# Moving VectorE's modulation products one place up in its order, and the split of one output weight ahead of the scores of heads 4 and 5

## The reference, cut to what matters

```python
c_act = jax.nn.silu(c)
mod = jnp.matmul(c_act, w_ada[l]) + b_ada[l]                  # 1024 -> 6 * 1024
sh_m, sc_m, gt_m, sh_f, sc_f, gt_f = jnp.split(mod, N_MOD, axis=-1)
h = modulate(rmsnorm(x, norm_mix_g[l]), sh_m, sc_m)
proj = jnp.matmul(h, w_in[l])
q, k, v, f_logit, u = jnp.split(proj, split_pts, axis=-1)
log_f = jax.nn.log_sigmoid(f_logit + b_fgate[l])
attn_out = forgetting_attention(q, k, v, log_f)   # logits + cumsum(log_f)[t] - cumsum(log_f)[s]
pool_out = multiscale_pool(u, w_pool[l], pool_scale[l])
mix = jnp.matmul(jnp.concatenate([attn_out, pool_out], -1), w_out[l])
x = x + gt_m[:, None, :] * mix
```

## Time and profile before

| | before |
|---|---|
| median of 3 runs | 771.52 us (771.48 to 771.83) |
| profiled execution, its own time | 771.5 us |
| its span | 769.7 us |
| TensorE matmul busy | 689.6 us (90%) |
| VectorE busy | 357.2 us (46%) |
| ScalarE busy | 295.3 us (38%) |
| read from HBM | 208.32 MB, 272 GB/s over the span |
| mean granted clock of TensorE | 0.972 |

### The profile page before, as it was taken

One profiled execution on the slowest core, in us unless ns is written; L12 is line 12 of the kernel. 1 busy time (PEld: TensorE's weight loads), 2 busy tenths in 40 slices (PEclk: granted clock), 3 DMA queues, 4 the chain that ended last, 5 costly groups with the idle time before them and its releaser, 6 DMA issues.

```text
span 769.7 us, 13061 instructions
## 1 busy us (share of the span) xinstructions
PE 689.6 (90%) x5482; PEld 538.5 (70%) x5482; DVE 357.2 (46%) x571; ACT 295.3 (38%) x432; POOL 46.5 (6%) x84
## 2 busy tenths in 40 slices
PE   3999999899757677778999999999999999999996
PEld 3887778743323122224999989998889999999995
DVE  3568861521110110105946885535675645555443
ACT  4244430331111010005764544678255643444432
POOL 0000000000000000000073750000000000000000
PEclk9999999999999898889999999999999999999999
DMA  8999899999999999999845234314345356554001
GB/s 354 408 418 391 318 424 419 422 421 421 424 422 424 422 421 426 403 413 424 308 181 218 113 126 181 134 64 156 110 170 185 135 195 219 219 196 185 3 1 55
DMA packets 33038, 210.27 MB, mean 273 GB/s; under 512 B 4688, under 2 KB 5072, under 8 KB 8656
## 3 DMA queue, kind: packets, MB, share of 16 engines
q1 hardware_dynamic: 32976, 209.38, 68.3%
HBM read 208.32 MB, written 1.05 MB: 272 GB/s over the span
## 4 chain that ended last, share of the span: by engine, by line
PE 70%; DMA 16%; DVE 5%; SPq 3%; ACT 3%; issue 1%; DVEq 0%; ACTq 0%
PE psum L419 69%; DMA raw<-in_w_exp 12%; DMA raw<-in_w_in_t 3%; SPq L459 2%; SPq L474 1%; PE psum L427 1%; DVE wlo L512 1%; ACT whi L495 1%; DMA raw<-in_w_ada_q 1%; DVE XL L1962 0%; DVE X L2398 0%; DVE acc L534 0%; ACT G L1283 0%; DVE XT L1310 0%; ACT XT L2342 0%
## 5 line engine op out<-in xcount | busy, mean ns | idle before, releaser
L419 PE MATMUL psum<-XH,whi 128*128 128x256 f32 x736 | 210.2, 286 | 4.3 <-DVE XL L665 2.8
L419 PE MATMUL psum<-XH,wlo 128*128 128x256 f32 x736 | 208.3, 283 | 0.0
L419 PE MATMUL psum<-XL,whi 128*128 128x256 f32 x736 | 208.0, 283 | 0.0
L512 DVE TENSOR_TENSOR wlo<-raw,whi 128x2048 fp32r<-128x2048 f32 (+1 forms) x88 | 168.9, 1957 | 48.6 <-ACT whi L495 48.6
L495 ACT ACTIVATE whi<-raw 128x2048 fp32r<-128x2048 f32 (+1 forms) x79 | 139.4, 1802 | 38.9 <-PE psum L419 22.4
L419 PEld LDWEIGHTS psum<-XH,whi 128*128 128x128 f32 x736 | 139.2, 189 | 8.0 <-issue 3.5
L419 PEld LDWEIGHTS psum<-XH,wlo 128*128 128x128 f32 x736 | 138.8, 189 | 0.0
L419 PEld LDWEIGHTS psum<-XL,whi 128*128 128x128 f32 x736 | 138.6, 188 | 0.3
L419 PE MATMUL psum<-raw,G 128*32 128x512 f32 x456 | 67.7, 682 | 20.3 <-DMA raw<-in_w_exp 20.2
L419 PEld LDWEIGHTS psum<-raw,G 128*32 128x32 f32 x456 | 17.7, 123 | 57.5 <-issue 56.6
L1267 ACT ACTIVATE WT<-psum 128x256 f32<-128x256 f32 x8 | 3.1, 383 | 134.4 <-PE psum L419 98.6
(11 more groups left out here) (350 smaller groups left out, 947.1 us busy)
## 6 DMA issues: line engine op xcount, KB each, us to landing
raw<-in_w_exp SPq DMA_DIRECT2D x85, 1024.0 KB, 23.1
raw<-in_w_ff SPq DMA_DIRECT2D x32, 1024.0 KB, 5.3
raw<-in_w_in SPq DMA_DIRECT2D x22, 1024.0 KB, 6.5
raw<-in_w_ada SPq DMA_DIRECT2D x16, 1024.0 KB, 11.7
raw<-in_w_in_t SPq DMA_DIRECT2D x8, 1024.0 KB, 18.4
X<-in_w_exp SPq DMA_DIRECT2D x5, 1024.0 KB, 24.9
raw<-in_w_ada_q SPq DMA_DIRECT2D x4, 1024.0 KB, 17.3
raw<-in_w_out_t SPq DMA_DIRECT2D x4, 1024.0 KB, 9.8
```

The lines of the kernel that those rows point to most:

```text
L419: return e.matmul(o, l, r, start=start, stop=stop, skip_group_check=True)
L512: e.tensor_tensor(wlo[j % NS][:, x], ring[slot[i]][:, x], whi[j % NS][:, x], ALU.subtract).then_inc(*steps_(("lo", j, x.start // 1024), *[ ...
```

## The change: what it does

On VectorE, the second product of block 4 now stands directly behind the first, before the forget gate's `lt`. The first product of block 5 takes the place that it leaves, behind the copies of `cum`; the second product of block 5 takes the place of the first, behind the scores of heads 2 and 3. Piece 20's low part takes the last vacated place, before `dve_ada` of blocks 4 and 6, and piece 22's low part moves from behind the probabilities of heads 4 and 5 to the place before the scores of heads 4 and 5. On ScalarE, piece 22's high part moves ahead of the exponentials of heads 4 and 5. TensorE's and SyncE's lists are the same; no instruction is added or removed.

```diff
@@ act_mixer
             act_rows(e, ut, 0, mix_act, "u")
+            act_pieces(e, 23)
             act_soft(e, 4)
             act_soft(e, 5)
-            act_pieces(e, 23)
@@ dve_mixer
             dve_products(e, 4, 0)
+            dve_products(e, 4, 1)
             p = bank("flog")
@@
             e.tensor_tensor(FF[:, :, 8:16], pf, Fh[:, :, :], ALU.subtract).then_inc(*mix_dve(("read", "cum"), "FF"))
-            dve_products(e, 4, 1)
+            dve_products(e, 5, 0)
@@
             dve_scores(e, 3)
-            dve_products(e, 5, 0)
+            dve_products(e, 5, 1)
             dve_probs(e, 0)
             dve_probs(e, 1)
             dve_scale_probs(e, 2)
             dve_scale_probs(e, 3)
-            dve_products(e, 5, 1)
+            dve_pieces(e, 21)
             dve_ada(e, 4)
             dve_ada(e, 6)
-            dve_pieces(e, 21)
+            dve_pieces(e, 23)
             dve_scores(e, 4)
@@
             dve_scale_probs(e, 5)
-            dve_pieces(e, 23)
             dve_ada(e, 7)
```

## The result

The changed kernel takes 774.96 us (median of 9 runs, 772.85 to 777.23) against 771.52 us (771.24 to 772.03) before: the ratio is 1.0043, with a 95% interval of 1.0032 to 1.0053. It is slower by 3.4 us where 0.75 us was forecast, and outside the stated range. The spread was larger too: 4.4 us over these nine runs, where the kernel before had 0.8. (In later series the kernel before has medians of 771.9 to 772.0 us and spreads of 1.5 us over 10 runs and 1.8 and 3.0 us over 29.)

The account below looks back on a forecast made before the run. DMA engines were taken to bound the experts, TensorE to pace piece 56. A 2.14 us TensorE delay less a 1.4 us reserve gave +0.74 us, outweighing a 0.8 us transfer gain: 772.3 us, range 770.2 to 773.7.

Parts of the forecast that it names:

- What bounds the kernel: DMA engines set the experts' pace; TensorE sets it at piece 56, loaded when it finishes the first expert group.
- Part 1: Block 4's second product ahead of the forget gate waits for piece 16's landing at 55.7; TensorE stalls 1.87 us.
- Parts 2 to 4: Block 5's products and the moved splits: first product free, second adds 0.27 us, splits add nothing.
- What SyncE gains: Slots free earlier win 3.4 us in the mixer; 2.6 are lost again at piece 36, leaving 0.8 us.
- The reserve of 1.4 us: DMA slack at piece 56: it lands 6.2 us after issue, where idle engines need 4.8.
- The sum: At piece 56 the end moves by the later of 2.14 - 1.4 = +0.74 us and -0.8 us: +0.74.
- d: TensorE's delay when it releases piece 56's memory, at 158 us: 1.87 + 0.27 = 2.14 us.
- rival A: No reserve at piece 56, whole stall arrives: 773.7 us; or clock falls after the stall: 773.1. Chance 0.21.
- the clock below 1.00 ahead of 150 us: Sign of being wrong: TensorE's granted clock under 1.00 in 60 to 150 us of the profile after.
- C: Faster by all that SyncE wins, 3.4 us: 768.1 us, if TensorE does not pace pieces 36 and 56. Chance 0.05.
- B: Faster because the stall does not reach piece 56; gain held to the 1.4 us reserve: 770.1 us. Chance 0.08.
- D: Slots do not matter and the stall is absorbed: 771.5 us, no change; chance 0.66 together with the likeliest case.

Follow-up runs that it names:

- e3: Kernel before with only the splits of pieces 20 and 22 moved to the changed kernel's places: 774.41 us, ratio 1.0030.
- e7: Changed kernel with pieces 15 and 16 swapped in loading order, and the input weight split behind the gate's work: 771.90 us, ratio 0.9997.
- e10: Kernel before with two idle TensorE matmuls behind the first two gathers, so only piece 56 is late: 773.60 us, ratio 1.0017.
- e11: Kernel before with four idle TensorE matmuls behind the first two gathers: 775.61 us, ratio 1.0039.
- e5: Kernel before run again, unedited, for a second profile: 771.97 us, ratio 0.9995.
- e9: Changed kernel with two idle TensorE matmuls ahead of its wait for lf: 773.46 us, ratio 1.0019.
- e1: Changed kernel run again, unedited, for a second profile: 776.77 us, ratio 1.0053.
- e2: Changed kernel with pieces 20 and 22 back at their old places, so only the three products moved: 775.22 us, ratio 1.0044.
- e6: Changed kernel with the second product of block 4 placed behind lf: 771.60 us, ratio 0.9997.
- e4: Kernel before with seven extra VectorE products on scratch ahead of the forget gate's bias, no slot freed earlier: 775.64 us, ratio 1.0041.
- e8: Changed kernel with four idle TensorE matmuls ahead of its wait for lf: 775.35 us, ratio 1.0035.
- e12: Kernel of e7 with one more idle matmul in each of TensorE's two waits ahead of piece 56: 771.16 us, ratio 0.9989.

## Why the prediction was wrong

**What bounds the kernel: right.** The engines' pace in the experts, and one place at which TensorE sets it. The table bears the rule out: the end is the landing of piece 56 plus 605.9 us in 14 profiles, within 0.5.

**Part 1, the stall: right.** Landing of piece 16 at 43.10 + 12.2 = 55.3; `lt` behind four products; TensorE's wait 1.74 us, forecast 1.87. (All of this profile runs 0.37 us early, as its first issues do.)

**Parts 2 to 4: right.** `FR` was on time; block 6's wait grew from 0.20 to 0.47 us, the 0.27 us forecast; the reserves of part 4 held, and e3 shows what is behind them once one is gone. Piece 36 was issued at 93.53, with the 0.37 us of the profile's offset 2.06 us later than before, forecast 2.14.

**What SyncE gains: right.** 75 to 80 us went from 256 to 357 GB/s, 80 to 90 from 241 and 393 to 262 and 434, 90 to 95 only from 301 to 306. Piece 36 landed at 98.3, 1.3 us earlier than before, 0.9 without the offset (forecast 0.8). Between 95 and 140 us the engines then moved 398 GB/s, before 422, a loss of 2.6 us, the size that was forecast. e7 shows how little a gain can bring: of 3.1 us at piece 36, 1.3 reach piece 56.

**The reserve of 1.4 us: right in the profiles, not at the median.** e10, e11 and e5 measure it in their profiles, as 1.5, 1.4 and 1.4 us. At the median, e10 and e11 move almost as without it (1.6 and 3.6 us for 1.6 and 3.35): the reserve is there, but half-clock time near 154 us, which the prediction put at nothing, draws on the same 1.4 us.

**The sum: wrong, in the term d.** The step that failed is "d stays 2.14 us", with the sentence that stands beside it, that the clock "is 1.00 around all waits of the mixer", so that a fall was put as one case of rival A and priced at 0.8 us. Behind the stall alone it measured 2.0 to 3.4 us (e9 against the changed kernel). d has another term, the time that TensorE loses at half clock ahead of piece 56. It was 2.9 us behind the stall in e1, and some 1 us near 154 us in the changed kernel's own profile: from the ranking at 151.06 to the issue at 160.65 it took 9.6 us in place of 8.5. With it d at piece 56 is 2.7 us in the changed kernel's own profile and 6.25 us in e1, and the rule gives 2.7 - 1.4 = 1.3 and 6.25 - 1.4 = 4.85 us. Measured at the landing it is 1.8 and 4.95; the 0.5 us over in the first is piece 56 itself, with 5.3 us to land in place of 4.8.

Of the signs of being wrong, the clock below 1.00 ahead of 150 us did not show in that first profile, but it did in e1 and e2. The price was wrong for two reasons. First, and this could have been read before, I took 16% of 5 us from a mean over a stage (0.86 in the earlier trace rows); a mean over 50 us hides stretches in which the clock is at half, and TensorE's token matmuls then start every 0.43 us in place of 0.23, for several microseconds in a row (e1). Second, I judged the risk by one profile, in which nothing fell ahead of 200 us. Six profiles have no new delay of TensorE ahead of the gathers and the waits there left open (both of the kernel before, e6, e7, e10, e11); three of them have half-clock time near 154 us. Of the seven that come there late (changed, e1 to e4, e8, e9), all have it.

**The cause, as far as shown.** The clock behind the stall: in the four profiles with an unfilled wait for `lf` of 1.7 to 2.1 us, half-clock time at 60 to 70 us is 0, 3.4, 6.8 and 6.8 us; in the ten without it, or with it filled, it is 0 each time, and filling it took 1.5 us or more off the median (e9 against the changed kernel's 774.96). Without the stall the loss is gone (e6), and a stall without the slots brings it back (e4). At the median the change then costs 2.0 to 3.4 us by the half clock behind the stall, and 1.4 us by the stall itself together with what falls near 154 us. The Trainium skill, "TensorE: Matmul & The Clock Gate", section "Part 1: The HAM clock gate (the "warmup" mystery)", says that the clock is set by how busy the engine has been of late, and that the same kernel has more or fewer slow matmuls at its start from run to run. e9 against e1 agrees with the first, 0 against 6.8 us. The second, told there of a kernel's start, has its like here in the middle of one: 0 and 6.8 us behind the same wait in the two profiles of the changed kernel. What decides it in a given run is not shown here and stays open, and so does whether the change makes the fall near 154 us more frequent: it came in three of six profiles without a delay and in seven of seven with one, too few to tell.

**The rivals.** A gave the side, and both of its halves have something in them: a reserve that is worth little at the median, and a fall of the clock behind the new stall. Each was put too low alone (773.7 and 773.1 us, measured 774.96), and they were not added up. C had no run to speak for it. B's cap, a gain of 1.4 us at most, is what e7's profile shows once the stall is out (piece 56 lands 1.3 us earlier), though at the median e6 and e7 measured no change, which is D's figure.

## What to carry to other kernels

A stall can cost more than its own length on an engine whose clock answers to it: here a wait of 1.7 us cost 3.4 to 4.8 us at the median. Ask what stands behind the wait at half clock, and read that from stretches in which the profile shows a half-clock rate, not from a mean. A reserve found in one profile is the reserve of that run; where other runs spend it on something random, the median pays for a new delay nearly one for one (e10, e11). And before a product is moved into a hole in an engine's time, look up when its operand lands: here the hole of 3.2 us was long enough for 3.0 us of work, but it began 2.1 us before the operand landed.

## What the runs showed of the hardware

Waits of 1.7 to 2.1 us on TensorE were followed by 3.4 or 6.8 us at the lower clock in three profiles of four; two idle matmuls of 1.88 us in the same place (e9), and four of 3.59 us (e8), left it at 1.00. A wait of 1.53 us at 82 to 84 us (e3) left it at 1.00 too. Near 154 us waits of 0.84 and 1.16 us, 2.4 us apart, were followed by 3.4 or 6.7 us of it in ten of thirteen profiles; in the fourteenth (e12), where they were filled down to 0.22 us, there was none. The same 128x512 idle matmul took 0.90 us at full clock (3.59 us for four in e8) and 1.22 us in e11, where the clock rose on the way.
